# MLPs of a hybrid decoder step: Strassen sums of the second product carried on in PSUM and added to four output blocks

## The reference

```python
def ffn(h, w1, w2):
    return jnp.square(jax.nn.relu(h @ w1)) @ w2

hp = hp + ffn(rmsnorm(hp, norm_ffn[layer]), w_ffn1[layer], w_ffn2[layer])
```

## Time and profile before

| | |
|---|---|
| median of 3 runs | 2751.97 us (2749.49 to 2754.66) |
| the profiled execution | 2746.19 us, span 2744.5 us, granted PE clock 0.99 |
| busy | PE 2639.2 us (96%), DVE 1495.5 (54%), POOL 1447.0 (53%), ACT 946.2 (34%) |
| MLP of layer 0, Strassen part of the second product | about 1366.5 to 1667.3 us of the span, tile ends to 1727 |
| MLP of layer 1, the same | about 2379 to 2680 us, tile ends to 2725 |

### The profile page before, as it was taken

How to read it: one execution, slowest core, us unless ns; L and a number is a source line. 1 busy time by engine, 2 the same in 40 slices (tenths; PEclk the granted TensorE clock), 3 DMA queues, 4 the chain that set the end, 5 groups by cost and what they waited for, 6 DMA issues and landing times. The chain is left out here.

```text
span 2744.5 us, 54327 instructions
## 1 busy us (share of the span) xinstructions
PE 2639.2 (96%) x22779; PEld 2521.7 (92%) x22779; DVE 1495.5 (54%) x1849; ACT 946.2 (34%) x1644; POOL 1447.0 (53%) x912
## 2 busy tenths in 40 slices
PE   8999989999999999999999998899999999999988
PEld 8999978986777799999999998899998999999988
DVE  5112186775554317455576769327336554676677
ACT  4100044656666324333333332211134333334332
POOL 6332201100001456777688888443548777688884
PEclk9999999999999999999999999999999999999999
DMA  6111243320204623344554431311223435554331
GB/s 194 47 48 63 93 145 109 95 77 2 94 2 140 234 74 139 116 163 153 184 213 146 155 117 31 131 47 47 94 108 108 148 113 166 201 216 152 126 109 63
DMA packets 197276, 319.98 MB, mean 117 GB/s; under 512 B 10813, under 2 KB 125250, under 8 KB 193898
## 3 DMA queue, kind: packets, MB, share of 16 engines
q1 hardware_dynamic: 186586, 293.37, 32.1%
q0 software_dynamic: 4032, 14.68, 1.5%
q10 hardware_dynamic: 6416, 8.45, 0.9%
HBM read 228.99 MB, written 91.67 MB: 117 GB/s over the span
## 5 line engine op out<-in xcount | busy, mean ns | idle before, releaser
L932 PE MATMUL psum<-part_hi,whl 128*128 128x258 f32 x3136 | 515.2, 286 | 23.8 <-DVE xlo_plain L1204 14.7
L932 PEld LDWEIGHTS psum<-part_hi,whl 128*128 128x128 f32 x3136 | 438.5, 191 | 27.5 <-DVE xlo_plain L1204 15.4
L478 PE MATMUL psum<-xhi,whl 128*128 128x344 f32 x1776 | 329.2, 320 | 1.1 <-ACT vCs L1367 0.6
L908 PE MATMUL psum<-shi,whl 128*128 128x258 f32 x1920 | 324.4, 283 | 2.2 <-DVE xlo_plain L1167 2.2
L932 PE MATMUL psum<-part_lo,whl 128*128 128x258 f32 x1568 | 317.0, 284 | 0.0
L449 POOL TENSOR_TENSOR whl<-wraw,zeroc 128x1024 fp32r<-128x1024 f32 x62 | 121.3, 1957 | 354.3 <-PE psum L478 169.0
L478 PEld LDWEIGHTS psum<-xhi,whl 128*128 128x128 f32 x1776 | 288.3, 188 | 1.7 <-issue 1.7
L908 PEld LDWEIGHTS psum<-shi,whl 128*128 128x128 f32 x1920 | 271.6, 190 | 2.6 <-POOL whl L353 2.6
L908 PE MATMUL psum<-xhi,whl 128*128 128x258 f32 x1440 | 250.5, 286 | 10.0 <-ACT xlo_plain L1047 10.0
L932 PEld LDWEIGHTS psum<-part_lo,whl 128*128 128x128 f32 x1568 | 244.8, 191 | 0.0
L353 POOL TENSOR_TENSOR whl<-raw_even,whl 128x512 fp32r<-128x512 f32 x112 | 175.5, 1581 | 86.3 <-ACT whl L974 62.2
(11 more groups left out here) (519 smaller groups left out, 5509.9 us busy)
## 6 DMA issues: line engine op xcount, KB each, us to landing
part_raw<-b_spill SPq DMA_DIRECT2D x98, 516.0 KB
b_spill<-rows_H SPq DMA_DIRECT2D x78, 516.0 KB, 3.9
rows<-in_cache_cmp_kv SPq DMA_DIRECT2D x128, 128.0 KB, 2.6
raw_even<-in_w_ffn SPq DMA_DIRECT2D x16, 1024.0 KB, 6.5
out_even<-in_w_ffn SPq DMA_DIRECT2D x16, 1024.0 KB, 6.2
out_odd<-in_w_ffn SPq DMA_DIRECT2D x16, 1024.0 KB, 7.7
raw_odd<-in_w_ffn SPq DMA_DIRECT2D x14, 1024.0 KB, 7.2
wraw<-in_w_in_ab SPq DMA_DIRECT2D x26, 512.0 KB, 3.6
```

The lines of the kernel that those rows point to most:

```text
L478: last = pe.matmul(psum[:, 3 * bset + c, 0:TC], w, rhs[ah][:, k0 + k, c * TC:(c + 1) * TC], start=(k == 0 and n == 0), stop=(k == kn - 1 a ...
L908: last = pe.matmul(psum[:, 2 * pair + h, 0:QT], fast_weights(first, u, i, wh)[:, k, :], fast_operand(i, ah)[:, k, h * QT:(h + 1) * QT], st ...
L932: last = pe.matmul(psum[:, 2 * p + h, 0:QT], out_weights(first, n, wh)[:, k, p % 2, :], (part_hi, part_lo)[ah][x][:, k, h * QT:(h + 1) * Q ...
```

## The change

- Second product: the order of the products is (0, 4, 6, 1, 2, 3, 5). Only the products at places 0, 4 and 5 start PSUM afresh; the others add to what the banks hold (M0, M0+M4, M0+M4+M6, M0+M4+M6+M1; M2; M3, M3+M5). After each product DVE adds the banks to one of four output blocks, all in `xlo_plain`. In c = 0 the first four are copies. The joins on DVE and POOL are gone.
- Weight sums of the second product: the first that is needed (s2) now goes to a place of its own (`second_sum`) and is needed for the second product of a group, where it was needed for the third before.
- First product: POOL's order in each unit is low0, low1, low2, s1, low3, s3, s2, low4, s4, low5, low6. On ACT, at the start of each MLP, b1_2 stands ahead of t1, t2, t4 and x3.
- Tile ends: sum and product by the factor are written back to PSUM; the banks are free after the third operation (`f_h`) instead of the first (`f_res`). The same for the gMLP's first banks and the last tile.
- Smaller: at the end of unit 15 DVE makes a part's low part ahead of the last square; a wait for a spill in c = 0 is gone.

```diff
                 low(0, a11)
                 low(1, a22)
+                low(2, a12)
                 total("low1", a22, a21, a22, ALU.add)
+                low(3, a22)
                 total("s1", a21, a11, a21, ALU.subtract)
                 total("s3", a11, a22, a11, ALU.subtract)
-                low(2, a12)
-                total("low2", a12, a12, a11, ALU.subtract)
-                pool.wait_ge(v_pool, pool_at(layer, f"{u}.s4"))
-                low(3, a22)
                 low(4, a11)
+                total("s2", a12, a12, a11, ALU.subtract)
                 low(5, a12)
                 low(6, a21)
...
-                low(c, 1, 0)
-                low(c, 1, 1)
                 low(c, 0, 0)
                 low(c, 0, 1)
                 for g in range(2):
                     a11, a12, a21, a22 = blocks_[g]
-                    total(c, g, "low1", a22, a21, a22, ALU.add)
-                    total(c, g, "s1", a21, a11, a21, ALU.subtract)
-                    pool.wait_ge(v_pool, pool_at(layer, f"c{c}.low0_{g}"))
-                    total(c, g, "s3", a11, a22, a11, ALU.subtract)
+                    total(c, g, "low0", a11, a11, a21, ALU.subtract)
+                    if c == 0:
+                        pool.wait_ge(v_done, product_done(layer, 15, 0))
+                    total(c, g, "s3", second_sum(g), a22, a11, ALU.subtract)
                     low(c, 4, g)
...
-            pool.wait_ge(sD, dve_at(layer, "m6_4_3"))
-            pool.tensor_tensor(total_of(4), total_of(4), total_of(0), ALU.add).then_inc(v_pool, 1)
...
-                pool.tensor_tensor(out_total(1, p), out_total(1, p), out_total(6, p), ALU.add).then_inc(v_pool, 1)
-                pool.wait_ge(v_pool, pool_at(layer, f"C21_{p}"))
-                pool.tensor_tensor(out_total(6, p), out_total(6, p), out_total(3, p), ALU.add).then_inc(v_pool, 1)
...
-        ORDER = (1, 0, 4, 6, 3, 2, 5)
-        PARTS = ("T4", "B11", "T2", "T3", "T1", "B21", "B22")
+        ORDER = (0, 4, 6, 1, 2, 3, 5)
+        PARTS = ("B11", "T2", "T3", "T4", "B21", "T1", "B22")
...
+        BLOCK = {0: (0, 0), 4: (0, 1), 6: (1, 1), 1: (1, 0), 2: (0, 0), 3: (1, 1), 5: (0, 1)}
...
-                                                     start=(k == 0 and m == 0), stop=(k == 1 and m == 2))
+                                                     start=(k == 0 and m == 0 and o in (0, 4, 5)),
+                                                     stop=(k == 1 and m == 2), skip_group_check=True)
...
-                    pe.wait_ge(f_res, F0 + 8 * layer + q - 1)
+                    pe.wait_ge(f_h, F0 + 8 * layer + q - 1)
...
             high(1, 0)
             high(1, 1)
+            high(1, 2)
             sums_high(S_T1, "s1_3")
             sums_high(S_T2, "s2_3")
             sums_high(S_T4, "s4_3")
             act.wait_ge(n_acc, 7 * (2 * layer + 1))
             for k in range(4):
                 act.activation(ssum[:, S_T3, k, :], hT[:, k, HT:T], ACT.Copy, scale=gain[:, k:k + 1]).then_inc(sA, 1)
-            high(1, 2)
             first_relu(0)
             first_relu(1)
...
-                if j == 44:
-                    dve.wait_ge(sD, dve_at(layer, "m6_0_3"))
-                    event(dve.tensor_tensor(total_of(2), total_of(2), total_of(0), ALU.add))
-                if j == 45:
-                    dve.wait_ge(v_pool, pool_at(layer, "V"))
-                    event(dve.tensor_tensor(total_of(5), total_of(5), total_of(4), ALU.add))
-                if j == 46:
...
-                dve.tensor_tensor(thirds(row), thirds(row), pset(n % 2), ALU.add).then_inc(f_res, 1)
-                dve.wait_ge(f_res, F0 + 8 * layer + n + 1)
-                s, v = link("dve", dve.tensor_tensor(row, row, fwide[:, :], ALU.mult))
+                s, v = link("dve", dve.tensor_tensor(pset(n % 2), pset(n % 2), thirds(out_row(n)), ALU.add))
+                dve.wait_ge(s, v)
+                s, v = link("dve", dve.tensor_tensor(pset(n % 2), pset(n % 2), thirds(fwide[:, :]), ALU.mult))
                 dve.wait_ge(s, v)
                 dve.wait_ge(s_reload[p], 32 if layer == 0 else 64)
-                dve.tensor_tensor(hT[:, n, :], hT[:, n, :], row, ALU.add).then_inc(f_h, 1)
+                dve.tensor_tensor(thirds(hT[:, n, :]), thirds(hT[:, n, :]), pset(n % 2), ALU.add).then_inc(f_h, 1)
```

More of the change, by code:

```diff
@@ L391, in pool_out @@
             for c in range(7):
-                blocks_ = [[out_block(first, c, i, g) for i in (0, 2, 6, 1)] for g in range(2)]
-                low(c, 1, 0)
-                low(c, 1, 1)
+                blocks_ = [[out_block(first, c, i, g) for i in (0, 2, 3, 1)] for g in range(2)]
                 low(c, 0, 0)
@@ L408, in pool_out @@
                     a11, a12, a21, a22 = blocks_[g]
+                    total(c, g, "s3", a21, a21, a22, ALU.add)
+                for g in range(2):
+                    a11, a12, a21, a22 = blocks_[g]
                     low(c, 2, g)
[L410 to L431 removed]
+                    total(c, g, "low2", a12, a12, second_sum(g), ALU.subtract)
+                for i in (3, 5):
+                    for g in range(2):
+                        low(c, i, g)
+            for q in range(8):
+                plain_low(q)
             if layer:
[L433 removed]
+                row = out_row(KT - 1)
                 pool.wait_ge(n_R, 4)
[L435 removed]
+                pool.wait_ge(sD, dve_at(layer, "m6_3_3"))
                 pool.tensor_tensor(row, row, fwide[:, :], ALU.mult).then_inc(v_pool, 1)
@@ L697, in build @@
         CACHE_ROWS = (128 * NB + 256, 128 * NB)
-        ORDER = (1, 0, 4, 6, 3, 2, 5)
-        PARTS = ("T4", "B11", "T2", "T3", "T1", "B21", "B22")
+        ORDER = (0, 4, 6, 1, 2, 3, 5)
+        PARTS = ("B11", "T2", "T3", "T4", "B21", "T1", "B22")
         SUM_OF = {3: "s1", 4: "s2", 5: "s4", 6: "s3"}
         def act_mlp():
-            order = [f"x1_{k}" for k in range(4)] + ["b1_0", "b1_1", "t1", "t2", "t4"] + [f"x3_{k}" for k in range(4)]
-            order += ["b1_2", "r0", "r1", "b1_3", "q0", "b1_4", "b1_5", "q1"]
+            order = [f"x1_{k}" for k in range(4)] + ["b1_0", "b1_1", "b1_2", "t1", "t2", "t4"] + [f"x3_{k}" for k in range(4)]
+            order += ["r0", "r1", "b1_3", "q0", "b1_4", "b1_5", "q1"]
             for u in range(1, 16):
@@ L729, in dve_mlp @@
                 order += ["g0"] if u == 15 else []
-                order += [f"c12_{u}", f"square0_{u}", f"u3_{u}", f"c21_{u}", f"c22_{u}", f"square1_{u}"]
-                order += ["g1"] if u == 15 else [f"{x}_{u // 2}" for x in ("T1", "T2", "T4", "T3")] if u % 2 else []
+                order += [f"c12_{u}", f"square0_{u}", f"u3_{u}", f"c21_{u}", f"c22_{u}"]
+                order += ["g1"] if u == 15 else []
+                order += [f"square1_{u}"]
+                order += [f"{x}_{u // 2}" for x in ("T1", "T2", "T4", "T3")] if u % 2 and u < 15 else []
             for j in range(49):
@@ L737, in dve_mlp @@
                 order += {47: ["g49", "g50"], 48: ["g52"]}.get(j, [f"g{j + 2}"])
-                order += {86 // 2 + 1: ["e11"], 86 // 2 + 2: ["e12a"], 86 // 2 + 3: ["e12b"]}.get(j, [])
             return order
-        POOL_UNIT = ("low0", "low1", "s1", "s3", "s2", "low2", "s4", "low3", "low4", "low5", "low6")
-        POOL_OUT = ("low1_0", "low1_1", "low0_0", "low0_1", "s1_0", "s3_0", "s2_0", "low4_0", "s1_1", "s3_1", "s2_1",
-                    "low4_1", "low6_0", "low6_1", "low3_0", "low3_1", "low2_0", "s4_0", "low2_1", "s4_1", "low5_0", "low5_1")
+        POOL_UNIT = ("low0", "low1", "low2", "s1", "low3", "s3", "s2", "low4", "s4", "low5", "low6")
+        POOL_OUT = ("low0_0", "low0_1", "s3_0", "s2_0", "low4_0", "s3_1", "s2_1", "low4_1", "low6_0", "low6_1",
+                    "low1_0", "low1_1", "s1_0", "s1_1", "low2_0", "s4_0", "low2_1", "s4_1", "low3_0", "low3_1", "low5_0", "low5_1")
         def pool_mlp():
@@ L747, in pool_mlp @@
             order += [f"c{c}.{x}" for c in range(7) for x in POOL_OUT]
-            order += ["V", "plain0", "U3", "plain1", "plain2", "plain3", "C21_0", "C22_0", "plain4", "plain5"]
-            order += [f"{x}_{p}" for p in range(1, 4) for x in ("C21", "C22")]
-            return order + ["plain6", "plain7", "scaled", "with_residual"]
+            return order + [f"plain{q}" for q in range(8)] + ["scaled", "with_residual"]
         def act_at(layer, name):
@@ L1182, in dve_ffn @@
                 event(dve.tensor_tensor(hidden_block(u, 1, 1), part_u, copy5, ALU.add))
+                if u == 15:
+                    part_low(1)
                 after(u, "c22")
                 event(dve.scalar_tensor_tensor(hidden(u, 1), hidden(u, 1), 0.0, hidden(u, 1), ALU.max, ALU.mult))
-                if u == 15:
-                    part_low(1)
-                elif u % 2:
+                if u % 2 and u < 15:
                     hidden_sums(u // 2)
```

82 lines of the change are left out of this document (23 added, 59 removed).

## The result

The changed kernel takes 2755.99 us (median of 20 runs, 2750.56 to 2761.28) against 2748.86 us for the kernel before in the same runs: ratio 1.0031, interval 1.0023 to 1.0038. It is slower by 0.3%, some 8.5 us, where 10 us faster was forecast. The profiled execution took 2760.52 us, span 2758.7 us.

A forecast was written before the change was run, and what follows sets the result against it. PE, busy 96% of the span, was taken as the bound. Gains 22.9 + 9.5 + 2.0 = 34.4 us less a loss of 24.2 gave 10.2 us faster, 2742 us; own range 2728 to 2758.

The forecast's parts named there:

- Part 4: First product, POOL's new order in the other 28 units: s4 later, but 1.1 us of cover, so cost nothing.
- the first rival: First product: DVE's row sums slow POOL, copy1 1.1 us late in each of 28 units; net 21 us slower, 2773; 16%.
- Part 3: Start of each MLP, b1_2 ahead on ACT: called the largest loss, 12.1 us a layer, 24.2 us (17 to 37).
- part 5: Start of a second product: the wait for POOL goes or shrinks, gain 1 us each, bounds -2 to 1.3 each.
- Part 2: Tile ends of layer 0: DVE's operations in PSUM quicker, 59.75 to 49.5 us; gain 9.0 plus 0.5 us, bounds 5 to 11.5.
- part 1: Second product, joins gone: PE's waits for evictions and lower clock go, gain 22.9 us, bounds 18 to 24.
- likeliest case: Whole kernel: the forecast itself, 10.2 us faster, median 2742 us, given 61%.

The follow-up runs named there:

- run with fills: Changed kernel with DVE's four sums of hidden rows, in every second unit, replaced by zero fills: 2732.48 us, ratio 0.9949 to the kernel before.
- s4 early: Changed kernel with s4 directly behind s2, ahead of low4, on POOL in every unit: 2733.94 us, ratio 0.9950 to the kernel before.
- run with the start alone: Changed kernel with POOL's new order in unit 1 only, old order in units 2 to 15, b1_2 still ahead: 2734.55 us, ratio 0.9944.
- run with a short V: Kernel before with POOL's V, the sum DVE's second join waits on, cut to two columns of each row: 2739.79 us, ratio 0.9962.
- run with the tile ends alone: Kernel before with only the tile ends changed, sum and product back into PSUM: 2738.57 us, ratio 0.9961.

## Why the prediction was wrong

**Part 4, POOL's order in the other 28 units, is the step that failed.** It was put at nothing, with a cover of 1.1 us. It cost 11.4 and 12.3 us, 23.7 in all, and turned the sign; 0.85 us a unit in the mean, over the 0.4 that the first rival named as its turning point. What the term had wrong is the time of one POOL operation: it put all seven on the way to s4 at 1.36 us, with next to nothing for DVE's work beside them. The rival (the hidden-row sums slow POOL, copy1 comes late) is what happened in the main, though not in every unit, and with a second delay on DVE's side that neither it nor the forecast had. One unit with such sums beside it, in the changed kernel: POOL first, then DVE:

```profile
1155.57 6.77 POOL L352 TENSOR_TENSOR whl<-raw_even,whl 128x512 fp32r<-128x512 f32 x3
1162.30 1.28 POOL L357 TENSOR_TENSOR raw_even<-raw_even 128x512 f32<-128x512 f32 x1
1164.32 1.29 POOL L352 TENSOR_TENSOR whl<-raw_even,whl 128x512 fp32r<-128x512 f32 x1 [0.74 <-ACT whl L962]
1165.56 3.12 POOL L357 TENSOR_TENSOR raw_even<-raw_even 128x512 f32<-128x512 f32 x2
1169.43 1.35 POOL L352 TENSOR_TENSOR whl<-raw_even,whl 128x512 fp32r<-128x512 f32 x1 [0.74 <-ACT whl L962]
1170.75 2.27 POOL L357 TENSOR_TENSOR raw_even<-raw_even 128x512 f32<-128x512 f32 x1
```
```profile
1154.50 2.20 DVE L1135 TENSOR_TENSOR rows_H<-xhi_plain,rows_H 128x1032 f32<-128x1032 f32 x1
1156.73 2.21 DVE L1137 TENSOR_TENSOR rows_H<-xhi_plain,rows_H 128x1032 f32<-128x1032 f32 x1
1158.86 2.32 DVE L1138 TENSOR_TENSOR rows_H<-xhi_plain,rows_H 128x1032 f32<-128x1032 f32 x1
```

The first row holds low0, low1 and low2 of a unit: 2.26 us each beside DVE's sums, against 1.38 in rows 12. Behind them follow s1, low3, s3 with s2, low4 and s4, the last one slow again (2.27 us), beside DVE's square. Then ACT, from b2 to b5 and copy1, and PE:

```profile
1159.42 0.62 ACT L962 ACTIVATE whl<-raw_even 128x512 fp32r<-128x512 f32 x1
...
1173.05 0.63 ACT L962 ACTIVATE whl<-raw_even 128x512 fp32r<-128x512 f32 x1 [3.70 <-POOL raw_even L357]
1173.59 0.58 ACT L1035 ACTIVATE xlo_plain<-psum 128x516 f32<-128x516 f32 x1
...
1174.32 0.48 PE L895 MATMUL psum<-xhi,whl 128*128 128x258 f32 x2 [0.96 <-ACT xlo_plain L1035]
```

The way of part 4 was laid out rightly: it counted 11.1 us from b2's end to s4's end, and PE to need copy1 13.3 us after b2's end. Here b2 ends at 1160.04, s4 at 1173.02, 13.0 us later, and copy1 at 1174.17, 14.1 us after b2. That is 0.8 us past the need, and PE waits 0.96. The 1.9 us too much are the two slow operations, low2 and s4, 0.9 us each over the 1.36 that was put for them. Only low2 is beside the sums; s4 is beside the square (L1169, 2.21 us from 1169.67), and in the run with fills, where the square starts 0.6 us behind s4, s4 takes 1.75 us. The fault is the row that this came from: rows 12 are of one unit in which the pieces of this way are not beside the hidden-row sums, and its pitch was used for all 28. The sums come in every second unit, and it is every second unit that waits, six times a layer.

The two experiments take the lateness away at either end:

| from b2's end to s4's end, a unit with sums or fills | us |
|---|---|
| changed kernel | 13.0 (1160.04 to 1173.02) |
| with the fills, POOL's order the same | 11.4 (1152.14 to 1163.50) |
| with s4 early, the sums as before | 9.3 (1152.84 to 1162.14) |

In both the waits are gone, so the stall needs both, the later s4 and the slowed operations. The groups of POOL's low parts over some 245 us of layer 0 (line, operation, shapes, count, busy us, mean ns), first in the changed kernel, then with s4 early, then with fills:

```profile
L352 POOL TENSOR_TENSOR whl<-raw_even,whl 128x512 fp32r<-128x512 f32 x42 | 71.2, 1702 | 17.0 <-ACT whl L962 16.6
```
```profile
L352 POOL TENSOR_TENSOR whl<-raw_even,whl 128x512 fp32r<-128x512 f32 x42 | 71.0, 1700 | 16.9 <-ACT whl L962 16.9
```
```profile
L352 POOL TENSOR_TENSOR whl<-raw_even,whl 128x512 fp32r<-128x512 f32 x42 | 55.3, 1323 | 31.1 <-ACT whl L962 31.1
```

1.70 us with the sums and 1.32 without them: this is the contention, and moving s4 doesn't take it away. These rows are of the weights in `raw_even`, the units with sums beside them; the low parts of the other units (`raw_odd`) take 1.48, 1.65 and 1.32 us in the three runs, so with s4 early POOL's low parts are slower in the mean than in the changed kernel, and the waits are gone all the same.

The six waits of 0.96 us make 5.8 of the 11.4 us in layer 0. The wait for the hidden part (L1150) makes 2.5 more, 3.72 us where the kernel before has 1.22; both experiments bear on it, 3.1 us with s4 early and none among PE's longer waits with the fills, so it hangs on DVE's sums, which take 2.12 + 2.20 + 2.21 + 2.32 = 8.85 us beside POOL's low parts, and 2.10 + 2.35 + 1.23 + 1.23 = 6.9 in the kernel before. The wait comes only once a layer because there, between the sums and L1150, DVE also has the reciprocal of the norm factor (in unit 2 alone):

```profile
1115.11 6.59 DVE L1145 RECIPROCAL fwide<-fwide 128x1032 f32<-128x1032 f32 x1
```

Together this is the added idle time, (313.10 - 303.61) - (301.71 - 300.49) = 8.3 us. The last 3.1 us are busy time, 303.6 against 300.5 us for the same 2473 matmuls. Half of it stands behind the longer wait, at a lower clock. The 5.6 us after it in the changed kernel, then the 5.6 us after one of the 0.96 us waits:

```profile
1122.40:1128.00 5.60, 5.60 (x34) 5.60 (x35) 3.21 (x4) 1.06 (x2) 3.14 (x3) 0.70 0.01 3
...
1174.40:1180.00 5.60, 5.60 (x47) 5.60 (x48) 0.00 (x0) 2.57 (x5) 3.78 (x4) 1.00 0.48 132
```

After 3.72 us the granted clock is 0.70 and 34 matmuls are done, 5.60 - 34 x 0.1207 = 1.5 us lost; after 0.96 us no clock is lost. Most of the other 1.5 us lies at the short waits all the same: the next one ends at 1216.05, 41.73 us after the one at 1174.32, where two units take 2 x 20.27 = 40.54 us. So a wait of 0.96 us costs 1.2 us, and six of them 1.4 us more than their idle time.

**Part 3, the start with b1_2 ahead on ACT: right, and in size.** 12.1 us a layer were forecast (its own terms add up to 12.3), 11.9 came. The two stalls stand where they were said to be:

```profile
1070.01 0.77 PE L895 MATMUL psum<-xhi,whl 128*128 128x258 f32 x2 [8.38 <-DVE fwide L621]
...
1084.49 0.77 PE L895 MATMUL psum<-xhi,whl 128*128 128x258 f32 x2 [6.01 <-ACT xlo_plain L1035]
```

8.38 us for `n_ms`, where 2074.8 - 2066.2 = 8.6 was computed, and 6.01 before the third product. POOL's five operations on the way to copy1, here low3, s3 with s2, low4 and s4:

```profile
1071.28 1.94 POOL L352 TENSOR_TENSOR whl<-raw_even,whl 128x512 fp32r<-128x512 f32 x1 [7.75 <-ACT whl L962]
1073.18 5.05 POOL L357 TENSOR_TENSOR raw_even<-raw_even 128x512 f32<-128x512 f32 x2
1078.97 1.60 POOL L352 TENSOR_TENSOR whl<-raw_even,whl 128x512 fp32r<-128x512 f32 x1 [0.74 <-ACT whl L962]
1080.53 1.71 POOL L357 TENSOR_TENSOR raw_even<-raw_even 128x512 f32<-128x512 f32 x1
```

Three of them were put at 1 us over 1.3, so 6.9 us, and take 7.0; two at 0.3 over, so 3.2, and take 3.3. Here contention was counted, from the right rows, and the term held; in part 4 it was not. The run with the start alone has the same 11.9 us a layer. What doesn't hold is its first sentence, by which one moved line is the largest loss: with that line put back and POOL's order kept, only 6.3 us a layer of the start came back, and 5.6 are POOL's order in unit 1. The line moved by itself, with POOL's old order, was not run.

**Parts 1 and 5, the second product: right in direction, too small by 5 us.** Forecast 22.9 + 2.0 = 24.9 us, of which 1.2 lay in the tile ends, so 23.7; measured 28.7 in the stretches, 24.6 by the difference of two runs, which is uncertain by some 5 us. PE's idle time fell from 300.73 - 288.27 = 12.5 us to 2.2 in layer 0, and its busy time from 288.3 to 284.2, 4.1 us a layer where I took 2.3 for the lower clock after the one long stall. Three things lie in the difference. First, a wait that the prediction left out, though it is longer than that for POOL in part 5: PE waits for the first copies of a second product. The kernel before, then the changed one:

```profile
PE psum L932 <- DVE xhi_plain L1197: 4.2, 2, 2.1
```
```profile
PE psum L919 <- DVE xlo_plain L1178: 2.5, 2, 1.3
```

It gave 0.8 us a layer, while the wait for POOL gave 0.3 (2.5 to 1.9 in two) where 1 was put. Second, the groups that the prediction called bound by matmuls were not quite: one group of 336 matmuls takes 40.75 us in the kernel before and 40.53 in the changed one, in the mean of six, without a wait in the list and at full clock. That is 1.3 us a layer; what it is stays open. Third, about 1 us a layer in small amounts around the waits that went. It is not the clock: in windows of 6 us over this stretch of the kernel before, the granted clock is 1.00 everywhere but in the two at the long stall (0.57 and 0.86). One later reading of mine was wrong, too: after the prediction I took most of the long stall for DVE's wait for V. The run with a short V shows 3.4 us a layer for it, of 14.3: the three joins held evictions back on DVE for 3.40 + 3.35 us and a third like them, and a wait removed from among them moved more than half of its worth into the next stall. That the whole gain needs all of this work gone is my reading of this one run; the joins were not taken out one by one. A matmul that adds to its bank at the start costs nothing that shows: 2354 matmuls in 284.19 us are 0.1207 us each, the pace of rows 13.

**Part 2, the tile ends: right.** Layer 0 went from 59.75 us to 1733.36 - 1683.99 = 49.4, forecast 49.5. With the 1.2 us counted in part 1, 10.7 us were forecast and 11.0 came. DVE in one tile of the changed kernel:

```profile
1706.86 1.24 DVE L1198 TENSOR_TENSOR psum<-psum,xlo_plain 128x1032 f32<-128x1032 f32 x1 [0.58 <-PE psum L938]
1708.14 1.24 DVE L1200 TENSOR_TENSOR psum<-psum,fwide 128x1032 f32<-128x1032 f32 x1
1709.41 1.23 DVE L1203 TENSOR_TENSOR hT<-hT,psum 128x1032 f32<-128x1032 f32 x1
1710.56 1.28 DVE L549 SCALAR_TENSOR_TENSOR xlo<-hT,small,xhi 128x1032 fp32r<-128x1032 f32 x1
```
```profile
1733.36 0.39 PE L524 MATMUL psum<-whl,xhi 128*128 128x256 f32 x1 [2.80 <-DVE hT L1203]
```

The product by `fwide` takes 1.24 us against 3.34, the low part 1.28 as put, and DVE waits for PE (0.58) instead of PE for DVE. The uncovered end of tile 7 is the 2.80 us. This is where the rule of the Trainium skill's "VectorE: DVE Perf Modes", section "Rules for kernel authors", was weighed: for elementwise work on a matmul's output, either to accept the speed of a PSUM source or to copy to SBUF first if many operations follow. The measurement decides against the copy here. While POOL works in SBUF, staying in PSUM made the operation 2.1 us shorter. The run with the tile ends alone, 10.7 us, has the same size.

**The sum.** With part 4 at its measured 23.7 us the forecast would have been 13.5 us slower. The second product gave 5.0 us more than put, the tile ends 0.3 and the start 0.4; that leaves 8. The likeliest case and its sign were wrong for one term.

The measured median, 2755.99 us, still lies inside the stated range of 2728 to 2758, and this is luck. The range was made of gains of 27 to 37 us and a loss of 18 to 31; the stretches show gains of 39.6 and a loss of 47.5, both outside, and they cancelled. (From those bounds the lower end comes out as 2731, not 2728.)

## What to carry to other kernels

When a queue is reordered, follow the chain of the element that others wait for through every kind of iteration, not through one clean one: here every second unit has DVE sums beside it, and that unit decides. A cover of 1 us on a chain of seven operations, each of which can take 1.3 or 2.3 us, is no cover, and its price is paid per unit. Ask of each edit in a bundle what it is worth by itself: here the moves in two queues cost some 47 us and hid 35 us or more of gain, and the stall at V was worth 3.4 us a layer, less than the wait of 5.72, while the work behind it stayed.
